# A two-layer decoder trunk: the condition vector is loaded as columns, and VectorE takes the parameters after its first four modulation units

## The reference

```python
def ada_modulate(c, w, b):
    m = jax.nn.silu(c) @ w + b
    shift, scale, gate = jnp.split(m, 3, axis=-1)
    return shift[:, None], scale[:, None], gate[:, None]

def reference(x, c, ...):                      # x (1, 256, 2048), c (1, 2048), all float32
    for i in range(2):
        shift, scale, gate = ada_modulate(c, ada_w[i, 0], ada_b[i, 0])
        h = rms_norm(x, norm_g[i, 0]) * (1.0 + scale) + shift
        mix = even_mixer(h, ...) if i % 2 == 0 else odd_mixer(h, ...)   # attention layers
        x = x + gate * mix
        shift, scale, gate = ada_modulate(c, ada_w[i, 1], ada_b[i, 1])
        h = rms_norm(x, norm_g[i, 1]) * (1.0 + scale) + shift
        x = x + gate * conv_ffn(h, ffn_w_up[i], ffn_conv_w[i], ffn_conv_b[i], ffn_w_down[i])
    return x
```

## Time and profile before

| | |
|---|---|
| median of 3 runs | 2056.01 us |
| profiled execution, first to last instruction | 2054.0 us |
| PE busy | 1889.3 us, 92% |
| VectorE busy | 1559.5 us, 76% |
| ScalarE busy | 1057.0 us, 51% |
| DMA moved | 521.25 MB, mean 254 GB/s |
| first sums of the modulation done | at 115.6 us of the span |

### The profile page before, as it was taken

The page is one execution under the profiler, slowest core; times in us unless marked ns, Lnnn a source line. Parts: engine busy times, 40 slices in busy tenths (PEclk is TensorE's granted clock), DMA queues, the critical chain, the costliest instruction groups (busy, mean ns, idle before and its releaser), DMA issues.

```text
span 2054.0 us, 34033 instructions
## 1 busy us (share of the span) xinstructions
PE 1889.3 (92%) x11434; PEld 1629.2 (79%) x11434; DVE 1559.5 (76%) x2447; ACT 1057.0 (51%) x2257; POOL 220.1 (11%) x317
## 2 busy tenths in 40 slices
PE   3279998889999999999999999989999999999998
PEld 2158854766799999997877878777799999998787
DVE  4988744777778888889887888788677777778554
ACT  1145446655544545555544456565455555556443
POOL 2220001552100000000011000043000000000000
PEclk9689998999999999999999999999999999999999
DMA  8979985567588888886997886868567777765555
GB/s 325 399 278 320 339 295 170 198 229 245 200 278 281 270 273 277 278 272 231 331 332 266 271 282 203 301 220 300 193 232 224 225 234 235 224 203 177 177 189 176
DMA packets 210967, 521.25 MB, mean 254 GB/s; under 512 B 23041, under 2 KB 43010, under 8 KB 186018
## 3 DMA queue, kind: packets, MB, share of 16 engines
q1 hardware_dynamic: 180722, 316.19, 47.3%
q0 software_dynamic: 28032, 201.44, 26.9%
q10 hardware_dynamic: 2096, 2.12, 0.3%
HBM read 517.53 MB, written 2.12 MB: 253 GB/s over the span
## 4 chain that ended last, share of the span: by engine, by line
PE 73%; DVE 13%; DMA 9%; ACT 3%; issue 1%; SPq 0%; DVEq 0%; POOLq 0%; ACTq 0%
PE ps L1039 12%; PE ps L1035 12%; PE ps L1036 12%; PE ps L931 10%; PE ps L927 10%; PE ps L928 10%; DVE acc L1712 6%; DVE ring_lo L1790 3%; DMA ring<-in_od_w_in 2%; DMA first_ring<-in_ada_w 2%; DMA ring<-in_ev_w_in 1%; DMA aring<-in_ada_w 1%; PE ps L761 1%; PE ps L1131 1%; DVE L L1947 1%
## 5 line engine op out<-in xcount | busy, mean ns | idle before, releaser
L1242 ACT ACTIVATE ring_hi<-ring 128x512 fp32r<-128x512 f32 (+2 forms) x1152 | 690.8, 621 | 595.5 <-DMA ring<-in_ffn_w_up 231.6
L1790 DVE TENSOR_TENSOR ring_lo<-ring,ring_hi 128x512 fp32r<-128x512 f32 (+2 forms) x1152 | 742.3, 680 | 283.1 <-ACT ring_hi L1242 281.4
L1035 PE MATMUL ps<-hT_hi,ring_hi 128*128 128x256 f32 x2048 | 512.2, 283 | 1.5 <-PE ps L1039 0.7
L1036 PE MATMUL ps<-hT_lo,ring_hi 128*128 128x256 f32 x2048 | 507.2, 280 | 0.0
L1036 PEld LDWEIGHTS ps<-hT_lo,ring_hi 128*128 128x128 f32 x2048 | 387.3, 189 | 0.0
L1035 PEld LDWEIGHTS ps<-hT_hi,ring_hi 128*128 128x128 f32 x2048 | 384.7, 188 | 2.3 <-issue 1.2
L1039 PE MATMUL ps<-hT_hi,ring_lo 128*128 128x256 f32 x2048 | 329.2, 282 | 2.4 <-DVE ring_lo L1790 2.4
L1039 PEld LDWEIGHTS ps<-hT_hi,ring_lo 128*128 128x128 f32 x2048 | 279.2, 187 | 2.6 <-DVE ring_lo L1790 2.6
L1712 DVE SCALAR_TENSOR_TENSOR acc<-aring,cs,acc 128x2048 f32<-128x2048 f32 x112 | 263.4, 2352 | 20.6 <-DMA aring<-in_ada_w 8.8
L928 PE MATMUL ps<-ring_hi,hT_lo 128*128 128x512 f32 (+2 forms) x640 | 243.8, 382 | 0.0
L643 POOL DMA_DIRECT2D aring<-in_ada_w x176 | 94.4, 536 | 1380.7 <-DVE acc L1712 1355.6
(11 more groups left out here) (244 smaller groups left out, 1996.4 us busy)
## 6 DMA issues: line engine op xcount, KB each, us to landing
aring<-in_ada_w POOLq DMA_DIRECT2D x176, 1024.0 KB, 6.9
ring<-in_ffn_w_up SPq DMA_DIRECT2D x512, 256.0 KB, 3.0
ring<-in_ffn_w_down SPq DMA_DIRECT2D x256, 256.0 KB, 3.1
ring<-in_od_w_in SPq DMA_DIRECT2D x112, 256.0 KB, 3.5
ring<-in_ev_w_in SPq DMA_DIRECT2D x80, 256.0 KB, 5.8
first_ring<-in_ada_w POOLq DMA_DIRECT2D x16, 1024.0 KB, 7.2
ring<-in_ev_w_out SPq DMA_DIRECT2D x64, 256.0 KB, 3.5
ring<-in_od_w_out SPq DMA_DIRECT2D x64, 256.0 KB, 4.0
```

Source lines behind the costliest of these rows:

```text
L1035: nc.tensor.matmul(o[q], hi, hT_hi[:, kt, :], start=start, stop=False, skip_group_check=True)
L1036: nc.tensor.matmul(o[q], hi, hT_lo[:, kt, :], start=False, stop=False, skip_group_check=True)
L1242: ins = nc.scalar.activation(out_, in_, f, **kw)
L1790: put(v.tensor_tensor(ring_lo[:, g, part], ring[:, g, part], ring_hi[:, g, part].bitcast(F32), ALU.subtract), lo_ok)
```

## The change

The condition vector leaves the rows. SP loads it straight into `cs`, 128 partitions by 16 columns, by one transfer whose single elements are 4 bytes, each 512 bytes from the next one of the same partition. It stands where the load of the 16 rows stood, first on SP. ScalarE waits for that transfer alone and takes silu in place. VectorE waits for silu and does the first four modulation units, and what it did ahead of them (the copies into `prm`, the mask row, the three gains) stands in a function `parameters()` that is called behind them, ahead of the wait for `cb_mm`.

```diff
-for _name, _n in (("c", KT), ("norm_g", 4 * KT), ("nsa_g", 2), ("dsa_g", 2), ("nope_g", 2),
+for _name, _n in (("norm_g", 4 * KT), ("nsa_g", 2), ("dsa_g", 2), ("nope_g", 2),
...
-            row_load(0, ROWS["c"][0], c.rearrange("o (k p) -> (o k) p", p=P))
+            sp.dma_start(cs[:, :], c.rearrange("o (k p) -> p (o k)", p=P), allow_slow_non_contiguous=True).then_inc(c_in, 16)
...
-            act.wait_ge(prm_ok.handle, 4)
-            run(cs_ok, cs[:, :], prm[:, ROWS["c"][0]:ROWS["c"][0] + KT], ACT.Silu)
+            act.wait_ge(c_in, 16)
+            run(cs_ok, cs[:, :], cs[:, :], ACT.Silu)
...
-            dve.wait_ge(prm_T.handle, 1)
-            for a, b in ((0, ROWS_A), (PE_COL, PE_COL + 2 * CMP_BLOCK), (CW_COL, 4 * P), (4 * P, PRM)):
-                put(v.tensor_copy(prm[:, a:b], ps[:, a // 512, a % 512:a % 512 + b - a]), prm_ok)
-            dve.wait_ge(rev_mm.handle, 1)
-            put(v.tensor_tensor(rev, ps[0:SLOTS, 2, 0:REV], negrow, ALU.add), rev_ok)
-            lane.after()
-            for j, (name, sc) in enumerate((("nsa_g", HD ** -0.5), ("dsa_g", HD ** -0.5), ("nope_g", (HD + ROPE) ** -0.5))):
-                put(v.tensor_scalar(gs[:, j:j + 1], prm[:, ROWS[name][0]:ROWS[name][0] + 1], sc, None, ALU.mult))
-            dve.wait_ge(cs_ok.handle, 1)
+            def parameters():
+                ...                                  # the same lines, without the wait for cs_ok
...
+                dve.wait_ge(cs_ok.handle, 1)
                 one_pass(0)
+                parameters()
                 dve.wait_ge(cb_mm.handle, 1)
```

More of the change, by code:

```diff
@@ L354, in trunk_program @@
         rows_in = sem("rows_in")
+        c_in = sem("c_in")
         landed = [sem(f"landed{s}") for s in range(RING)]
@@ L1694, in put @@
                 lane.done(ins, sig_ if sig_ is not None else dve_s)
-            dve.wait_ge(prm_T.handle, 1)
-            for a, b in ((0, ROWS_A), (PE_COL, PE_COL + 2 * CMP_BLOCK), (CW_COL, 4 * P), (4 * P, PRM)):
-                put(v.tensor_copy(prm[:, a:b], ps[:, a // 512, a % 512:a % 512 + b - a]), prm_ok)
-            dve.wait_ge(rev_mm.handle, 1)
-            put(v.tensor_tensor(rev, ps[0:SLOTS, 2, 0:REV], negrow, ALU.add), rev_ok)
-            lane.after()
-            for j, (name, sc) in enumerate((("nsa_g", HD ** -0.5), ("dsa_g", HD ** -0.5), ("nope_g", (HD + ROPE) ** -0.5))):
-                put(v.tensor_scalar(gs[:, j:j + 1], prm[:, ROWS[name][0]:ROWS[name][0] + 1], sc, None, ALU.mult))
-            dve.wait_ge(cs_ok.handle, 1)
+            def parameters():
+                dve.wait_ge(prm_T.handle, 1)
+                for a, b in ((0, ROWS_A), (PE_COL, PE_COL + 2 * CMP_BLOCK), (CW_COL, 4 * P), (4 * P, PRM)):
+                    put(v.tensor_copy(prm[:, a:b], ps[:, a // 512, a % 512:a % 512 + b - a]), prm_ok)
+                dve.wait_ge(rev_mm.handle, 1)
+                put(v.tensor_tensor(rev, ps[0:SLOTS, 2, 0:REV], negrow, ALU.add), rev_ok)
+                lane.after()
+                for j, (name, sc) in enumerate((("nsa_g", HD ** -0.5), ("dsa_g", HD ** -0.5), ("nope_g", (HD + ROPE) ** -0.5))):
+                    put(v.tensor_scalar(gs[:, j:j + 1], prm[:, ROWS[name][0]:ROWS[name][0] + 1], sc, None, ALU.mult))
             def mod_unit(m, t, col, extra=0):
```

## The result

The changed kernel takes 2064.19 us (median of 20 runs, 2059.04 to 2074.14), the kernel before 2056.32 us in the 20 runs beside them. The ratio is 1.004, with a 95% interval of 1.0027 to 1.0053: slower by 5.6 to 10.9 us. Two executions in a slow state count for no ratio of this document, one of 6660.68 us of the kernel before here and one of 3132.39 us of the kernel with the transfer of `c` alone. The profiled execution has a span of 2062.8 us, 8.8 more than before. The forecast was 2064.3.

A forecast was written before the change was run, and what follows sets the result against it. Bound: the start's chain from the parameter loads (`ropeg`) through PE to `cb_mm` and pass 1. PE's start +9.1, early units 0, copies 0, silu 0, pass 2 -0.8: +8.3, so 2064.3 us; range 2055 to 2069.

The forecast's parts named there:

- the term of -0.8: Pass 2 loses its excess because the Toeplitz load no longer shares the engines with its loads: -0.8 us (0 to -1.9).
- The early units' move is worth 0: VectorE's first four units start earlier, but `cb_mm` still stands between them and pass 1: 0 us.
- `c` is nearly free: The new `c` transfer's 2048 single elements, at 25 ns each, take 3.2 us (0 to 6.7); landed by some 6 us.
- VectorE ready at about 8 us: After the `c` transfer, silu's table load and silu, VectorE is ready before the first unit's load lands at 11.5 us.
- Idle stretches of VectorE of some 8 and some 10 us: Expected signs: VectorE idles some 8 us ahead of the copies and some 10 us ahead of `cbias`.
- Units at 11.5, 15, 18, 21.2; loads at 14.6, 17.9, 21.1, 24.3: First four `ada_w` loads land at the first times; VectorE's finished units let GpSimd issue loads 4 to 7 at the second.
- q0 and q1 in turn, one for one: Each of about 640 short q1 packets waits behind an 8 KB q0 packet; q0 runs until 31.2 to 32.8 us.
- The rival by the Trainium skill: At 9 to 17 descriptors a turn, parameters are not held up: 2054 to 2056 us, chance 0.17.
- `ropeg` lands at 32.0: The last parameter load, which PE's start waits for, lands 9.1 us later than 22.91 (31.3 to 33.7).
- PE does not start cold: Nine more idle microseconds leave PE's clock up; the cold rival had up to `cb_mm` doubled: 2080 us, chance 0.03.
- A shift of the sums passes on to the end: Behind PE's last partition sums lies unmoved PE work, so a shift of their end moves the kernel's end.
- x is covered: x, behind the parameters on q1, lands by 38 us, ten microseconds before `cb_mm`; its squares stay off the chain.

The follow-up runs named there:

- x first: Changed kernel with `w2`, `b2` and `ropeg` out of PE's starting wait, and x issued ahead of those three loads: 2059.28 us, 1.0009 against the kernel before.
- the last kernel: Kernel of "use the idle stretch" with the Toeplitz reload issued ahead of x's squares and VectorE's wait for the late three behind the loop: 2052.73 us, 0.9973.
- use the idle stretch: Kernel of "x first" with pass 1 also done ahead of VectorE's wait for `cb_mm`: 2055.72 us, 0.9999 against the kernel before.

## Why the prediction was right, step by step

The mechanism was right. That the time came out within 0.1 us is luck: the interval of the loss is 5.6 to 10.9 us wide, the changed kernel's executions reach from 2059 to 2074, and the term of -0.8 was right by chance, as told below.

- *The early units' move is worth 0.* Right. VectorE's idle time ahead of `cbias` in the changed kernel is 12.04 us; x first, with PE at 23.80, gives 1.0009 in spite of the early units.
- *`c` is nearly free.* Right, and too dear at 25 ns an element. From 2 to 3 us q1 moved 1422 packets in 78.4% of 16 engine-us, which is 8.8 ns each; the transfer took 3.0 us to landing and was there at 3.9, not at 6. The rule of the Trainium skill ("DMA: Bandwidth & Descriptors", "Rules for kernel authors"), one descriptor for each element of a non-contiguous last dimension, agrees with the number of packets: up to 60 us q1 had 5346 in the changed kernel and 3314 before, 2032 more, which is 2048 elements in place of 16 rows. But no harm came of it: `c` alone measured 0.9993. The 0 to 0.7 us of displacement were no part of the loss either: `ropeg` landed at 23.01 with `c` alone and at 22.38 with the loads held back, against 22.91.
- *VectorE ready at about 8 us.* The number was right by luck, the reason wrong. Silu was done at 5.4; VectorE waited until 7.58 for the load of `ada_b`. It cost nothing, since the first `ada_w` load landed at 11.5 only.
- *Idle stretches of VectorE of some 8 and some 10 us.* They were 10.54 and 12.04. The forecast's own times gave about that (units through at 23.6 and transposes at 33.9, and L852 with its 12.91 us behind them); the two figures in it were mis-worked and are in no sum.
- *Units at 11.5, 15, 18, 21.2; loads at 14.6, 17.9, 21.1, 24.3.* Measured: 11.55, 15.02, 17.72, 21.39; 14.60, 18.01, 20.74, 24.39. They depend on the landings of the first four loads alone, which did not move.
- *q0 and q1 in turn, one for one.* Right: 576 to 577 from 20 to 31 us. The rival by the Trainium skill ("DMA: Bandwidth & Descriptors", "Queues, rings and completion order"), with 9 to 17 descriptors a turn, was weighed too loosely: with so many on either side of a turn the counts would come out one for one as well, and `ropeg` as late; only short turns of q0 beside long ones of q1 give the rival's 2054 to 2056. What contradicts the figure of the Trainium skill here is the order of the single packets told above, 921 neighbours of 976 from different queues. The measurement of the earlier trace rows decided for the forecast, and rightly, since the sum needs the counts alone.
- *`ropeg` lands at 32.0.* It landed at 32.40: 9.5 us later than before and 0.4 later than taken, inside the 31.3 to 33.7.
- *Pass 1 at 53.2.* Measured 53.57, the same 0.4 on.
- *Pass 2 gives back 0.8.* The size was off in its parts. Passes 2 and 3 took 9.87 and 9.88 us against 10.75 and 10.80, 1.8 us back, twice the term; the Toeplitz load did land in 7.7 us instead of 14.7. Pass 4 then took 10.74 against 10.33, and pass 7 lost 0.4 as well. From pass 1 to the sums 0.9 us came back (9.46 later at one, 8.54 at the other). The term of -0.8 was right by luck, as a net of two effects that it did not hold; why the later passes lost, no run here tells. The sum came out at +8.5 instead of +8.3.
- *PE does not start cold.* Right: the granted clock was 1.00 over 32.5 us of idleness, and behind them the transposes took 1.71 us (1.74 before) and L852 the same 12.91.
- *A shift of the sums passes on to the end.* Right in this pair: 8.5 us at the sums, 8.7 at `cw_now`, 8.8 in the span. The first projection started at 124.38 and 133.00, and from there to `cw_now` it took 437.6 and 437.7 us. But over the twelve profiled executions this stretch took from 434.5 to 442.4 us, and the medians of the other kernels do not follow their sums: 3.0 to 3.8 us later gave 0.37 to 0.42% (some 8 us), and 4.7 us earlier gave nothing. So one pair of spans could not have shown the step; the loss of the changed kernel rests on its 20 executions and on the kernel that holds the loads back.
- *x is covered.* Right: the forecast had it landed by 38, and it landed at 37.2. The cover was what it had been before, by ScalarE's wait for VectorE's sum, with the squares and a table load already behind it (kernel before, then changed):

```profile
40.07 0.20 ACT L1242 ACTIVATE xst<-xst 128x2 f32<-128x2 f32 x1 [4.85 <-DVE xst L1775]
```

```profile
49.54 0.20 ACT L1243 ACTIVATE xst<-xst 128x2 f32<-128x2 f32 x1 [4.94 <-DVE xst L1779]
```

x and `cb_mm` had both moved by some 9.4 us. What the forecast did not say is that this cover goes as soon as `cb_mm` alone comes back by 8 us; then x is the wait.

## What to carry to other kernels

Starting a consumer earlier also frees its buffers earlier, and then long transfers go out sooner. Before you move it, list what those transfers will stand in front of. Look too at the next wait behind the moved work: where it hangs on something else, as `cb_mm` does here on the parameter loads, the early start is worth nothing, and only its side effects are left. Where two queues take turns as these do (576 packets to 577), count packets, not bytes: the queue of 512-byte packets advanced at the pace of the 8 KB ones. If the short ones are urgent, hold the long ones back by one wait (0.9992 here), or make them shorter (1.0011). To turn an early start into time, the work must also pass the wait that had made the old order cheap, and the last kernel is the only one here in which a gain is clear of the noise.

## What the runs showed of the hardware

- A transfer of 2048 single elements of 4 bytes, with no other queue at work from 2 to 3 us, took 8.8 ns a packet and 3.0 us in all.
- The same 2 MB in 1 KB packets took 7.7 us to landing alone (the changed kernel), 14.7 beside 8 KB loads for a part of its way, 27.2 in the kernel before with pass 1 ahead, and 43 to 45 us when they never stopped, at 16.4% of the engines' time in "use the idle stretch".
- q0 and q1 changed turns packet by packet: 512-byte packets of q1 and 8 KB ones of q0 stood next to each other; 921 of 976 pairs of neighbours were of different queues.
- Two executions of one kernel had spans of 2055.9 and 2066.1 us, at mean granted clocks of 0.976 and 0.967. A single profile's span can't settle a difference of 0.2%; its rows up to the sums could, since that pair agrees there within 0.9 us.
